# Five stages of a hybrid diffusion layer as one program per engine, with turned part sums and head norms in four groups

## What is computed

```
mods = silu(cond) @ w_ada + b_ada                       # 6 x 2048, for context and for latent
h = rms(x) * (1 + scale1) + shift1
z, xbc, dt, q, k, v, pool, gates = split(h @ w_in)
merged = sum_i sigmoid(gates_i) * (branch_i @ w_i_out)  # ssd scan, attention, pooling
x += gate1 * (merged @ w_out)
h2 = rms(x) * (1 + scale2) + shift2
x += gate2 * moe(h2)            # 16 experts in 4 groups of 4, top 2 of the best group
y = rms(x)
# in the attention: q, k = rms over each head of 64, then rotary on the latent tokens
```

## Time and profile before

| | |
|---|---|
| median of three runs | 2038.62 us (2035.18 to 2040.0) |
| the profiled execution | 2038.76 us, span 2037.0 us |
| PE busy, weight loads busy | 97%, 85% |
| DVE, ACT, POOL busy | 72%, 48%, 0% |
| mean granted clock of PE | 0.984 |
| HBM read | 455 MB, 225 GB/s over the span |

### The profile page before, as it was taken

One profiled execution on the slowest core, in us unless ns is written; L12 is line 12 of the kernel. 1 busy time (PEld: TensorE's weight loads), 2 busy tenths in 40 slices (PEclk: granted clock), 3 DMA queues, 4 the chain that ended last, 5 costly groups with the idle time before them and its releaser, 6 DMA issues. The chain is left out here.

```text
span 2037.0 us, 27648 instructions
## 1 busy us (share of the span) xinstructions
PE 1979.8 (97%) x10684; PEld 1728.6 (85%) x10684; DVE 1470.6 (72%) x2106; ACT 984.1 (48%) x1468; POOL 7.1 (0%) x11
## 2 busy tenths in 40 slices
PE   7899999999999999999999999998999999999996
PEld 2199988987888999999999999986888888888884
DVE  1468676548888777775677874344799997999997
ACT  1233465332445332222333233333778887888883
POOL 0000000000000000000000000000000000000000
PEclk9999999999999999999999999996999999999998
DMA  9944333342444455555255566446799998999992
GB/s 375 388 157 148 119 123 130 114 153 104 161 145 155 166 197 207 202 199 183 95 209 204 206 223 217 165 144 212 282 384 366 360 358 285 360 357 365 363 358 113
DMA packets 133513, 460.95 MB, mean 226 GB/s; under 512 B 17568, under 2 KB 23520, under 8 KB 133248
## 3 DMA queue, kind: packets, MB, share of 16 engines
q1 hardware_dynamic: 133376, 459.12, 62.9%
HBM read 455.06 MB, written 4.00 MB: 225 GB/s over the span
## 5 line engine op out<-in xcount | busy, mean ns | idle before, releaser
L186 ACT ACTIVATE whi<-raw 128x1024 fp32r<-128x1024 f32 x640 | 678.8, 1061 | 767.1 <-PE bank L217 632.3
L192 DVE TENSOR_TENSOR wlo<-raw,whi 128x1024 fp32r<-128x1024 f32 x640 | 778.2, 1223 | 360.7 <-ACT whi L186 330.9
L212 PE MATMUL bank<-hhi,whi 128*128 128x384 f32 x1408 | 482.3, 343 | 4.7 <-PEq L1036 1.8
L213 PE MATMUL bank<-hlo,whi 128*128 128x384 f32 x1408 | 472.8, 336 | 0.0
L212 PEld LDWEIGHTS bank<-hhi,whi 128*128 128x128 f32 x1408 | 265.7, 189 | 21.9 <-issue 18.1
L217 PE MATMUL bank<-hhi,wlo 128*128 128x384 f32 x1408 | 272.8, 334 | 0.0
L213 PEld LDWEIGHTS bank<-hlo,whi 128*128 128x128 f32 x1408 | 266.1, 189 | 0.8
L274 DVE SCALAR_TENSOR_TENSOR cond_parts<-raw,cond_padded,cond_parts 128x512 f32<-128x512 f32 x360 | 250.6, 746 | 0.8 <-DVE rstd L71 0.2
L217 PEld LDWEIGHTS bank<-hhi,wlo 128*128 128x128 f32 x1408 | 246.9, 188 | 0.0
L2243 PE MATMUL bank<-whi,pair_tokens 128*128 128x512 f32 x512 | 201.9, 394 | 0.7 <-issue 0.7
L2244 PE MATMUL bank<-whi,pair_tokens 128*128 128x512 f32 x512 | 200.8, 392 | 0.0
(11 more groups left out here) (338 smaller groups left out, 2228.1 us busy)
## 6 DMA issues: line engine op xcount, KB each, us to landing
raw<-in_dense SPq DMA_DIRECT2D x448, 512.0 KB, 4.5
raw<-in_moe SPq DMA_DIRECT2D x384, 512.0 KB, 5.3
cs_rows_bc<-cs_rows SPq DMA_DIRECT2D x8, 768.0 KB, 5.1
merged<-in_x SPq DMA_DIRECT2D x4, 768.0 KB, 10.5
x_again<-in_x SPq DMA_DIRECT2D x4, 768.0 KB, 7.1
out_y<-y_normed SPq DMA_DIRECT2D x3, 768.0 KB, 4.3
shift_rows<-cs_rows SPq DMA_DIRECT2D x2, 1024.0 KB, 8.8
pool_w_sb<-in_pool_w SPq DMA_DIRECT2D x1, 1024.0 KB, 7.1
```

Of the source, the lines that this page charges most:

```text
L186: self.nc.scalar.activation(self.whi[:, k % W, :], self.raw[:, n % R, :], ACT.Copy).then_inc(self.hi_done, 1)
L192: self.nc.vector.tensor_tensor(self.wlo[:, k % W, :], self.raw[:, n % R, :], self.whi[:, k % W, :].bitcast(F32), ALU.subtract).then_inc(se ...
L212: self.nc.tensor.matmul(out, self.whi[:, s, c], xhi[:, k, :], start=(k == 0), stop=False)
L213: self.nc.tensor.matmul(out, self.whi[:, s, c], xlo[:, k, :], start=False, stop=False)
```

## The change

`Phase` keeps the five functions of a stage, one per engine, and the state of the tile counters. `run` writes one block in which each engine goes through all stages given to it. The three merge stages, the output stage and the experts are one such block; `mix_phase` is a block of its own, and the barrier behind it stays. Where the barriers kept order, named waits stand: HeadsSplit, Pooling and out_phase wait for the last tile of the stage before (`used`) or the last merge, PE waits for the last tanh and merge before it writes banks 0 and 1.

`part_fold` goes. `part_turn` transposes the four pieces of one of the two groups into bank 7, `part_sum` lets ACT copy them with an accumulated sum into `part_sums`, `part_bias` adds the bias. A chunk's two halves come at o = 1 and 2 of the next round, and the last chunk of a stage in the next stage. The sums of the head norms use four column groups of the array, in batches after blocks 3, 7 and 9, the spreading four row groups; the selector is loaded four times. Branches of the code that no stage used (parts on POOL, `ada_row`) are dropped.

```diff
+def run(nc, phases):
+    with nc.Block() as block:
+        @block.tensor
+        def _(pe):
+            for phase in phases:
+                phase.begin()
+                phase.tensor(pe)
...
-def part_fold(N, pe, p):
+def part_turn(N, pe, p, g):
     pe.wait_ge(N.s_part, 32 * (p - PART_CHUNKS[0] + 1))
-    pe.wait_ge(s_add, p)
+    pe.wait_ge(N.s_summed, part_half(p, g))
     for q in range(4):
-        for g in range(2):
-            last = N.nc.tensor.matmul(N.bank[6][:, 2 * q + g:2 * q + g + 1], N.parts[:, p % N.parts.shape[1], g, q * P:q * P + P],
-                                      N.ones[:, 0:1], start=True, stop=True)
+        last = N.nc.tensor.transpose(N.bank[7][:, q * P:(q + 1) * P], N.parts[:, p % N.parts.shape[1], g, q * P:q * P + P],
+                                     N.ident[:, :])
+    last.then_inc(N.s_turned, 1)
+
+def part_sum(N, act, p, g):
+    act.wait_ge(N.s_turned, part_half(p, g) + 1)
+    if g == 0:
+        act.wait_ge(N.ada_sems[2], p)
+    for q in range(4):
+        last = N.nc.scalar.activation(N.ada_rows[:, q * P:(q + 1) * P], N.bank[7][:, q * P:(q + 1) * P], ACT.Copy,
+                                      accum_out=N.part_sums[:, q, g:g + 1])
+    last.then_inc(N.s_summed, 1)
...
 def merge_phase (tensor, in the middle of a tile):
-                if o == 1 and i > 0:
-                    side.fold_free(pe)
-                    fold(i - 1)
+            if owed(i) and o in FOLD_AT:
+                part_turn(N, pe, N.ada0 + i - 1, FOLD_AT.index(o))
...
-            fold(iters - 1)
...
+            if s == 0:
+                pe.wait_ge(N.gate_read, N.m0 + 1)
+            if s == 2:
+                pe.wait_ge(N.out_read, N.m0 + 1)
...
 class Attention:
-        self.selt = keep("head_sel_t", [32, 10, P], F32)
+        self.selt = keep("head_sel_t", [P, 10, P], F32)
...
-            pe.wait_ge(self.s_sq, b + 1)
-            mm(B[4][0:32, 0:T], self.sel[:, b, :], self.sq[:, b % 2, :], start=(b == 0), stop=(b == 9)).then_inc(self.s_sqs, 1)
+            if b in (3, 7, 9):
+                pe.wait_ge(self.s_sq, b + 1)
+                for bb in range(b // 4 * 4, b + 1):
+                    last = mm(B[4][self.lanes(bb), 0:T], self.sel[:, bb, :], self.sq[:, (bb + 2) % 4, :], start=(bb < 4), stop=(bb >= 6))
+                last.then_inc(self.s_sqs, 1)
...
-                    mm(B[2 + b % 2][:, 0:T], self.selt[:, b, :], N.rstd[0:32, :], start=True, stop=True).then_inc(self.s_bc, 1)
+                    mm(B[2 + b % 2][:, 0:T], self.selt[self.lanes(b), b, :], N.rstd[self.lanes(b), :], start=True, stop=True)\
+                        .then_inc(self.s_bc, 1)
...
 class HeadsSplit (act; dve alike without the two waits):
+        act.wait_ge(self.attention.s_o, 8)
+        act.wait_ge(N.used, N.own(N.tile0))
         for j in range(8):
-            self.N.nc.scalar.activation(S["hi"][:, j, :], S["q"][:, j, :], ACT.Copy).then_inc(self.s_hi, 1)
+            N.nc.scalar.activation(S["hi"][:, j, :], S["q"][:, j, :], ACT.Copy).then_inc(self.s_hi, 1)
+            if j == 3:
+                yield from hold(2)
         yield
     def pe(self, pe):
-        yield
+        yield from hold(3)
         pe.wait_ge(self.s_lo, 8)
...
 class Pooling (sp; pool alike):
+        sp.wait_ge(N.used, N.own(N.tile0 - 2 * POOL_BLOCKS))
...
 def out_phase (sync, gpsimd, scalar, vector, tensor):
+        sp.wait_ge(N.used, N.own(own[0]))
...
+                sp.wait_ge(split.s_done, KB)
...
+        pool.wait_ge(split.s_done, KB)
...
+            if s < 2:
+                part_sum(N, act, ada0 - 1, s)
...
+            if s == 1:
+                part_bias(N, dve, ada0 - 1)
+                dve.wait_ge(N.ada_sems[2], ada0)
+                V.scalar_tensor_tensor(out=N.mod_a[:, :, :], ...)
...
+            if s == 0:
+                pe.wait_ge(N.gate_read, N.m0 + 1)
+                pe.wait_ge(N.ada_sems[2], ada0 - 4)
...
-    merge_phase(N, N.S["hi"], N.S["lo"], True, "ssd", attention, parts="dve")
+    ssd = merge_phase(N, N.S["hi"], N.S["lo"], True, "ssd", attention)
...
+    run(nc, (ssd, heads, pooled, out, experts))
```

More of the change, by code:

```diff
@@ L1062, with merge_phase @@
 SPLIT_AT = 36288
-def merge_phase(N, ohi, olo, first, name, side=None, lead=0, parts=None, split=None):
+FOLD_AT = (1, 2)
+def merge_phase(N, ohi, olo, first, name, side=None, lead=0, split=None):
     nc, body = N.nc, len(MERGE_ORDER)
@@ new lines, in owed, with sync, gpsimd, scalar @@
+    def owed(i):
+        return N.ada0 + i > PART_CHUNKS[0]
+    def sync(sp):
+        beside = side.sp(sp)
+        for n in range(N.tile0 - lead, N.tile0 + iters * body):
+            N.load(sp, n + R)
+            next(beside, None)
+        for _ in beside:
+            pass
+    def gpsimd(pool):
+        side.pool(pool)
+    def scalar(act):
+        beside = side.act(act)
+        for s in range(lead):
+            N.act_hi(act, 0, 0, s - lead)
+            if s % 2 == 1:
+                side.evacuate(act, s // 2, N.tiles_done(0, 0, s - lead))
+            next(beside, None)
+        for i, t, kind, o in slots:
+            if kind == "ada":
+                continue
+            N.act_hi(act, i, body, t)
+            if o % 3 == 2:
+                m = i * 4 + o // 3
+                act.wait_ge(N.out_read, N.m0 + m + 1)
+                act.wait_ge(N.used, N.own(N.tile(i, body, t)))
+                nc.scalar.activation(gt[:, :], gate_bank, ACT.Tanh, scale=0.5).then_inc(N.gate_read, 1)
+            if split and o % 3 == 1 and i * 4 + o // 3:
+                split.high(act, i * 4 + o // 3 - 1)
+            for _ in range(side.steps(12 * i + o)):
+                next(beside, None)
+            if owed(i) and o in FOLD_AT:
+                part_sum(N, act, N.ada0 + i - 1, FOLD_AT.index(o))
+        for _ in beside:
+            pass
@@ new lines, in vector, with merge, condition @@
+    def vector(dve):
+        st = N.steps(dve)
+        beside = side.dve(dve, st)
+        def merge(i, t, o):
+            m = i * 4 + o // 3
+            dve.wait_ge(N.gate_read, N.m0 + m + 2)
+            dve.wait_ge(N.used, N.tiles_done(i, body, t))
+            acc = N.merged[:, m, :]
+            nc.vector.scalar_tensor_tensor(out=acc if first else mt[:, :], in0=gt[:, :], scalar=1.0, in1=out_bank,
+                                           op0=ALU.add, op1=ALU.mult).then_inc(N.out_read, 1)
+            if not first:
+                dve.wait_ge(N.out_read, N.m0 + m + 2)
+                add = nc.vector.tensor_tensor(acc, acc, mt[:, :], ALU.add)
+                if split:
+                    add.then_inc(split.s_done, 1)
+                else:
+                    st.chain(add)
+        before = None
+        def condition():
+            for i in range(iters):
+                for n in range(4 * ADA_BODY):
+                    part_add(N, dve, nc.vector, i, body, n)
+                    yield
+        adding = condition()
+        for s in range(lead):
+            N.dve_lo(dve, 0, 0, s - lead)
+            next(beside, None)
+        for _ in range(PART_STEPS[2]):
+            next(adding, None)
+        for i, t, kind, o in slots:
+            if kind == "ada":
+                continue
+            N.dve_lo(dve, i, body, t)
+            if before:
+                merge(*before)
+            before = (i, t, o) if o % 3 == 2 else None
+            if split and before and i * 4 + o // 3:
+                split.low(dve, i * 4 + o // 3 - 1)
+            for _ in range(side.steps(12 * i + o)):
+                next(beside, None)
+            if owed(i) and o == FOLD_AT[1] + 1:
+                part_bias(N, dve, N.ada0 + i - 1)
+            for _ in range(PART_STEPS[o % 3]):
+                next(adding, None)
+        merge(*before)
+        for _ in beside:
+            pass
@@ L1516, in pool @@
     def pool(self, pool):
-        self.N.nc.gpsimd.memset(self.pad[:, :, :, :], 0.0).then_inc(self.s_zero, 1)
+        N = self.N
+        pool.wait_ge(N.used, N.own(N.tile0 - 2 * POOL_BLOCKS))
+        N.nc.gpsimd.memset(self.pad[:, :, :, :], 0.0).then_inc(self.s_zero, 1)
     def evacuate(self, act, b, done):
```

1784 lines of the change are left out of this document (859 added, 925 removed).

## The result

The changed kernel takes 2011.78 us (median of 4 runs, 2010.0 to 2016.07); the kernel before took 2036.9 beside it (4 runs, 2034.74 to 2040.0). The ratio is 0.9879, 95% interval 0.986 to 0.9897: 1.2% faster. Over everything that was run later the medians are 2012.3 (8 runs, 2010.0 to 2016.1) and 2036.8 (55 runs, 2031.2 to 2044.2), 24.5 us apart. The forecast was 2017.2 with a range of 2010 to 2028. The profiled execution of the changed kernel has a span of 2010.0 us, 27.0 less than before.

A forecast was written before the change was run, and what follows sets the result against it. TensorE was taken to bound the merge stages, except a norm stretch set by VectorE. Borders 5.1, folds 9.6 and head norms 6.9 sum to 21.6 us off 2038.76, giving 2017.2, range 2010 to 2028.

The forecast's parts named there:

- The borders' pauses and waits: Three merge borders: barrier pauses, slow clock and a wait for heads removed, new named waits of 2.4 us added.
- The price of a fallen clock: Behind two merge borders PE runs at half clock for some 3 us: 1.6 us, together 3.2 removed.
- Merging alone: All four stage borders: 7.5 us removed, 2.4 added by named waits, 5.1 net less.
- The last border: Between output stage and experts PE waits 1.6 us for DVE's slot arithmetic and the barrier; this goes.
- Rival 5: Last routing steps: without the pause PE's clock could come back earlier, up to 8 us more gain, 2009.2; chance 0.05.
- One of its signs: Profile after the change: granted clock 1.00 in the 10 us behind each border.
- Turned sums: Condition chunks: 12 folds, 21.6 us, become 24 half turns of 0.5, 12.0; net 9.6 less (7.2 to 11.0).
- rival 4: ACT's sums end late, its weight splits too, and PE stops 1.5 us in 24 tiles: 2053; chance 0.05.
- Head norms: Ten sums of squares at 0.99 us each become three batches at 0.99: 6.9 us less, lower bound 1.8.
- rival 3: DVE's full norm stretch eats the gain ahead of it: 6.9 us back, 2024.1; chance 0.1.
- Rival 1: Head norms: the sums of squares run in series, 5.1 us back, 2022.3; chance 0.12.
- (2): Borders: named waits hold PE as long as the barriers did and the clock falls again, 4.8 back, 2022.0; chance 0.2.

The follow-up runs named there:

- E4: Changed kernel with all four stage borders separated again, folds and norms as changed: 2018.33 us, ratio 0.9902 to the kernel before.
- E9: Changed kernel with old folds, single sums of squares and five separate blocks, all three parts undone: 2035.85 us, ratio 0.9999 to the kernel before.
- E10: Changed kernel with old folds and single sums of squares, but still one merged program with named waits: 2027.01 us, ratio 0.9956 to the kernel before.
- E3: Changed kernel with a border of its own ahead of the expert stage only: 2014.12 us, ratio 0.9881 to the kernel before.
- E1: Changed kernel with turned part sums undone, one fold of 16 one-column matmuls per condition chunk: 2021.39 us, ratio 0.9915 to the kernel before.
- E2: Changed kernel with the ten sums of squares sent one by one, each still into its own 32 columns: 2019.21 us, ratio 0.9907 to the kernel before.
- E8: Changed kernel with nine idle products of 384 columns in the norm stretch, where PE waited: 2010.29 us, ratio 0.9865 to the kernel before.
- E12: Changed kernel run and profiled once more, no edit: 2013.52 us, ratio 0.9886 to the kernel before.
- E11: Changed kernel with nine idle products in the norm stretch and no PE wait for the last merge before the first output tile: 2010.33 us, ratio 0.9871.
- E7: Changed kernel with 18 idle products ahead of the last four condition tiles of the router's gap: 2012.69 us, ratio 0.9885 to the kernel before.

## Why the prediction was right, and where it fell short

**The borders' pauses and waits: right.** Forecast 3.5 net at A, B and C; measured from before to after 4.2 (121.95 - 115.11, less three chunks at 0.89). The price of a fallen clock, 1.6, and its place behind a pause were right (in E4 a tile whose sixteen products take 4.42 us for 2.8). The place as written, "right after a fold of 16 matmuls with one column and the idle gap", fits the kernel before. E4 shows that a fall can come without the fold; at the merge borders none came without a barrier. Merging alone, 5.1 in the forecast, is 5.8 by the table (the 4.2 and the last pause of 1.6), 6.0 by E4 and 8.8 by E9 to E10, whose barriers cost more than those of the kernel before.

**The last border: right in its pause, short in the pair of profiles.** 1.6 was forecast, E3 measures 1.39 in the trace and 1.8 in time. The first pair of profiles shows 8.65, and the rest is clock: 30.7 us low against 13.6. Rival 5 (0.05, "nothing dense is moved there") named this gain, but as a thing that the missing pause brings about, and it put the time at the lower level at some 16 us where the trace of before has 30.7. E3 has the pause and not the loss, E9 has all four borders and only 17.0 us of it. What the prediction didn't see is that these 30.7 us, which stood in its starting time of 2038.76, are an outcome that varies from one execution to the next. One of its signs failed here: it asked for a clock of 1.00 in the 10 us behind each border, and behind the fourth, where PE starts at 1381.30, the clock falls at 1386.4. Over the table, D goes from 36.53 us with 6.8 low to 47.15 with 30.7, about 0.4 us for each us at the lower clock (1.6 of the 10.6 is the pause). Whether the kernel before falls into the longest spells more often than the merged one, these profiles don't settle: 30.7 and 23.9 for it, 17.0 and 13.6 for E9 and E4 with their four borders, against 17.0, 17.1, 6.8, 13.6 and 17.0 for the merged ones without idle products (E10, E1, E2, and the changed kernel twice).

**Turned sums: right, a little low.** The step 24 x 0.5 = 12.0 was mis-sized: a half turn costs 0.45, so twelve chunks would give 10.7, not 9.6 (the bound was 11.0). Undone they bring back 8.8 in the table from ssd to out and 9.1 in time, since the chunk at A gives nothing (E1): a fold there would cover the wait for the heads, and the sum took the two as independent. Nor is the gain of the chunk in the stretch seen: that section takes 61.85 and 61.84 us before, 64.47 and 61.95 after. ACT's sums never hold PE (rival 4): between 541 and 1190 us of the changed kernel PE waits for another engine once, the 0.74 us for DVE at the first border. Its weight splits still wait for PE as in the earlier trace rows, in the row below (time line of ACT, changed kernel).

```profile
702.80 1.06 ACT L239 ACTIVATE whi<-raw 128x1024 fp32r<-128x1024 f32 x1 [3.10 <-PE bank L270]
```

**Head norms: right, and the disagreement with the rule settled.** 6.9 forecast, 6.90 by E2. From before to after the section shrinks by 7.33; where the other 0.4 come from is open. The first sign of failure, a stretch 2.6 us longer in the first profile, looked like rival 3 (DVE's full stretch eats the gain). DVE does set that stretch, but starts its root chain when the sums end, so it moved along; E8 and E12 show that the loss was clock: 61.74 us without a fall, 61.95 with one of 3.4 us (62.95 in E11), 64.47 with one of 10.2. E3, E4 and E7, with 6.8 to 10.2 us at the lower level there, have 64.5 to 64.6. Rival 1, sums in series, falls: four sums take 1.01 us.

**Where the 5.4 us are.** 2.0 is the base: the profiled execution took 2038.76, the median of 55 runs is 2036.8. 0.5 is the other end, 2011.8 in four runs and 2012.3 in eight. The other 2.9 (24.5 measured, 21.6 forecast) lie, by these profiles, mostly at the routing. From "sums" to "out" the table adds up to 948.06 us before, and to 929.40 and 926.82 in the two profiles of the changed kernel: 18.7 and 21.2 less, where 20.0 were forecast (21.6 less the 1.6 of the last border). By these profiles the medians leave 3.3 to 5.8 us for the start, D and the end, where 1.6 were forecast. D alone is 47.15 and 43.85 before, 38.50 and 40.00 after. Undone one by one from the changed kernel, merging, folds and sums give 6.0 + 9.1 + 6.9 = 22.0; with merging from E9 to E10 it is 8.8 + 9.1 + 6.9 = 24.8. Each of these is good to some 2 us, so neither sum proves that the parts add up to the last microsecond.

The range was said to hold two of the rivals together. That is so for (1) and (2), 2027.1; (2) and (3) give 2017.2 + 4.8 + 6.9 = 2028.9, 0.9 us outside. Nothing hung on it.

## What to carry to other kernels

A barrier costs its pause and often what the clock does behind it (here at one or two of three borders in each of five profiles); count both, and look in windows of 1 us. Before a difference between two profiles is given to a change, profile both kernels a second time: the first two differed by 27.0 us, the medians by 24.5, and single sections were off by 2.5 (stretch) and 3.3 us (D) from one execution of a kernel to the next. Read an experiment that is meant to keep the clock up in more than one trace too: E8's looked settled until E11. Cutting both traces at the same tiles gives terms good to a few hundredths in the sections without falls of the clock, where whole runs scatter by 10 us, and shows at once which sections repeat and which don't.

## What the runs showed of the hardware

**A busy PE can lose its clock.** In the kernel before, PE is busy without a break from 1404.02 to 1432, and at its lower level until 1424; in E7 the clock falls at 1382 with no idle time in front of it. Behind the sixteen condition passes the work there is small: products of 2, 128, 16 and 256 columns behind a weight load each, and in E7 products of 4 columns ahead of the fall. The Trainium skill ("TensorE: Matmul & The Clock Gate", Part 1) describes the clock as following how busy PE is, and takes its losses from idle gaps. The trace agrees that a gap can bring it down (E4's second border, not its first and third); these rows add that time recorded as busy does not by itself keep it up. The price by kind, at the upper and at the lower level: 24 products of 16 columns 2.82 and 5.14 us, eight folds of two columns 1.03 and 1.84. The upper one of the products, from E2:

```profile
1393.09 2.82 PE L2377 MATMUL bank<-half_gate_weights,pick 128*128 128x16 f32 x24
```

**The same code keeps or loses its clock around short waits.** In the norm stretch of the changed kernel the clock fell behind a wait of 1.07 us, for 10.2 us in one execution and 3.4 in the other, with the code and the time of arrival the same to 0.4 us. A wait of 0.89 us in the same stretch left it at 1.00 in E8 and was followed by a fall in E11. The two profiles of the kernel before have a longer wait there, 1.52 us and 1.51, and no fall in either:

```profile
490.00:500.00 10.00, 8.49 (x37) 6.31 (x38) 9.44 (x23) 1.06 (x1) 0.00 (x0) 1.00 0.25 93
```

So the length of one wait does not tell what the clock does, and what does is open. The same operations in the first profile of the changed kernel, at the lower level, and then in the second, at the upper:

```profile
484.29 2.29 PE L1355 MATMUL bank<-rstd,head_sel_t 32*128 32x384 f32 x4 [0.42 <-DVE q_heads L1464]
486.51 2.08 PE L1362 MATMUL bank<-q_heads,rope_swap 128*128 128x256 f32 x4
489.67 2.66 PE L270 MATMUL bank<-hhi,wlo 128*128 128x384 f32 x8
```

```profile
484.03 1.56 PE L1355 MATMUL bank<-rstd,head_sel_t 32*128 32x384 f32 x4
485.52 1.13 PE L1362 MATMUL bank<-q_heads,rope_swap 128*128 128x256 f32 x4
487.19 1.55 PE L270 MATMUL bank<-hhi,wlo 128*128 128x384 f32 x8
```

**Column groups run together although each loads weights into all 128 rows.** Four sums of squares in four groups of 32 columns take 1.01 us, one takes 0.99. In series they would have taken 3.18, the prediction's other bound. The weight-load rule that it cited ("TensorE: Matmul & The Clock Gate", Part 3, of the Trainium skill) does not hold for them; the same page's whole pack in about one matmul's time does. The dense stream shows the overlap already before the change: from 1040 to 1060 us PE and its weight loads of 128 rows are both busy for 20.00 of 20 us.
